# A hybrid encoder block on one core: expert rows gathered as U and V together, in segments of 1, 2, 3 and 2 tiles

## The chip, the cores and the metric

The kernel is one program on one core of a Trainium2 chip, with 128 partitions. Its time is the device time of one execution in microseconds. All data are float32. The engines are called PE (TensorE), DVE (VectorE), ACT (ScalarE), POOL (GpSimd) and SP (SyncE); each takes its own instructions in the order in which they are written, and they wait for each other through semaphores.

## What is computed

One layer on 1024 tokens of 1024 features: a gated linear attention and a sliding-window attention side by side, merged and projected, then a layer that retrieves experts by product keys, a gated embedding add and a last norm. Cut to what matters here:

```python
h = rmsnorm(x, norm_mix)
proj = h @ w_in                       # q, k, v, r, gate of one mixer, q, k, v of the other
x = x + (g_gla * y_gla + g_swa * y_swa) @ w_out
h = rmsnorm(x, norm_ffn)
# 8 heads: top 16 of 128 scores on two sides, top 16 of their 256 sums -> 16 experts e, gates g
u = take(u_tab, e)                    # 16384 x 1024 table
act = gelu(einsum('td,thkd->thk', h, u))
v = take(v_tab, e)                    # 16384 x 1024 table
x = x + einsum('thk,thkd->td', g * act, v)
x = x + sigmoid(rmsnorm(x, norm_ple) @ w_ple_gate) * (p @ w_ple_proj)
return rmsnorm(x, norm_final)
```

Each token takes 8 x 16 = 128 rows of U and 128 rows of V. These rows, 4 KB each, are 1074 MB in all, and each is used once.

## The kernel before

**Tiles, rows and steps.** A tile is 128 tokens, one on each partition; there are eight. For a tile, the k-th expert of a head is one gather of 128 rows (one per partition, 512 KB); a tile has 128 such rows of U and 128 of V. The whole program is laid on one axis of steps n. A step handles two rows, so a head is 8 steps, a tile 64, and all dots are done in steps 0 to 511. Every engine runs a loop over n with its own part of each step.

**A row of experts.** POOL gathers row `at` of U into one of six slots of ubuf and, ten steps later (VLAG), row `at` of V into one of eight slots of vbuf (line 431). DVE multiplies the U row with the tile's normed x in hbuf and sums it into a column of dots (`dot`, line 1133); that frees the slot of U. Once per head, at a step with n % 8 = 0, ACT takes the gelu of all 16 dots (line 877); DVE multiplies them with the gates' softmax (`weights`, line 1141). Ten steps after the dot the V row is added with its weight. Either DVE does it, in acc (line 1159), or PE does: ACT writes the weight on a diagonal (line 885, three buffers) and PE multiplies the diagonal with the V row into ysum in two halves of 512 columns (line 673). ON_PE says which: none in tile 0, the odd rows in tiles 1 to 6, all of tile 7; 512 rows on each. `second_residual` adds acc and ysum to x1 in tX (lines 1170 and 1175), at step 64i+9 for tile i-1.

**The indices** of a head come two heads ahead: `topk` is eleven pieces of DVE work at lines 1068 to 1096, spread over the steps, and ACT's exponential for the gates is at line 873.

**The front.** All before the experts is done for a segment at a time, in stages such as "gv0" (a quarter of v) or "ex1" (the exponentials of a batch of windows). SEGS = (1, 2, 2, 2, 1) tiles. 46 of the 51 weight pieces belong to it, each a slab of 1 MB that SP loads into a ring of three (line 370), PE multiplies with the segment's activations (`by_feature`, line 488, weights stationary; `by_token`, line 497, activations stationary) and ACT evicts from one of two banks (line 700 and others). Each segment loads its slabs anew. `plan()` gives each stage a step: the front of a segment is spread evenly over the steps up to 18 before its first dot, with some stages at least a step behind others (BEHIND). The last stages, wq0 to wq8, project the queries and find the 16 largest scores (`largest`, lines 975 to 981).

**The tail** of a segment (T0, T1, pg0 to pg3, pp, T2; the five other slabs) is the gated embedding add and the last norm. Tails of segments 0, 1 and 2 are hosted in the middle of the front of segments 2, 3 and 4 (HOSTED); those of the last two segments follow their last row, a stage a step.

**Order within step n.** PE: rows of V of step n-10, then the stages of step n. ACT: a gelu of a head if due, the gates' exponential if due, the stages of step n, then diagonals for the next step. DVE: dot, a piece of topk, dot, a piece of topk, the sums of step n-10, the vector parts of the stages of step n-1, weights if due, the norm of the next tile's hbuf (two buffers, line 1120). SP: x1 for hbuf 16 steps ahead of the tile, x1 for tX, then what stages need, then slabs up to step n+2.

## Time and profile before

| what | value |
|---|---|
| median of 3 runs | 3861.61 us (3858.42 to 3883.16) |
| the profiled execution | 3826.47 us |
| its span, first to last instruction | 3824.7 us |
| mean granted TensorE clock | 0.896 of full speed |
| busy: PE, DVE, POOL, ACT | 2919.9, 2603.0, 2337.5, 893.9 us |
| DMA | 1373.44 MB, mean 359 GB/s |

"Busy" counts an engine's instructions, not its waits. A row of a group gives the line, the engine, the operation, what it writes and reads, the count, the busy time and the mean of one, and then the idle time of the engine just before these instructions with what ended it ("issue" is a wait for nothing that the profile shows). The profile counts a float32 matmul twice, so two ysum matmuls of a row stand as four. The DMA share is the mean busy share of the core's sixteen DMA engines; it can go a little over 1, since packets overlap.

### The profile page before, as it was taken

The page shows a single profiled execution, that of the slowest core. Times are in us where ns is not written, and L with a number is a line of the kernel's source. Part 1 is how long each engine was busy: PE and PEld are TensorE (multiplying, and loading weights), DVE is VectorE, ACT ScalarE, POOL GpSimd, SP SyncE. Part 2 cuts the span into 40 slices and gives each one's busy share as a digit, 9 for nine tenths or more (in the row PEclk, how much of TensorE's full clock was granted, in tenths as well). Part 3 has the DMA queues.
Part 4 walks back from the last instruction along what each step waited for, and adds up shares of the span by engine and source line. Part 5 has one row for each costly group of instructions (what it writes and reads, how often), then busy time and mean ns, then how long its engine had stood idle before and what let it go on. Part 6 is the DMA issues. An engine that isn't in the chain of part 4 may idle for free.

```text
span 3824.7 us, 34537 instructions
## 1 busy us (share of the span) xinstructions
PE 2919.9 (76%) x11088; PEld 1913.1 (50%) x11088; DVE 2603.0 (68%) x5403; ACT 893.9 (23%) x1935; POOL 2337.5 (61%) x2052
## 2 busy tenths in 40 slices
...
GB/s 220 221 203 263 388 356 379 313 403 388 382 412 364 381 371 382 318 382 385 385 375 394 389 387 376 342 369 406 395 408 377 412 412 411 399 367 277 397 373 203
DMA packets 342549, 1373.44 MB, mean 359 GB/s; under 512 B 38737, under 2 KB 40657, under 8 KB 309730
## 3 DMA queue, kind: packets, MB, share of 16 engines
q0 software_dynamic: 294912, 1073.87, 72.9%
q1 hardware_dynamic: 47458, 297.36, 19.8%
...
## 4 chain that ended last, share of the span: by engine, by line
PE 16%; POOL 15%; issue 9%; DMA 7%; DVE 3%; another core or an unknown queue 2%; ACT 2%; ACTq 0%; DVEq 0%; POOLq 0%
POOL ubuf L431 8%; POOL vbuf L431 7%; PE ysum L673 7%; DMA vbuf<-in_v,idx 5%; PE bank L488 4%; PE bank L497 3%; DMA ubuf<-in_u,idx 1%; DVE ubuf L1133 1%; PE bank L660 1%; ACT diag L885 1%; DVE acc L1159 0%; PE bank L553 0%; DVE tX L1055 0%; PE wide L505 0%
## 5 line engine op out<-in xcount | busy, mean ns | idle before, releaser
L431 POOL DMA_INDIRECT ubuf<-in_u,idx x1024 | 1175.4, 1148 | 1054.0 <-DVE ubuf L1133 535.2
L673 PE MATMUL ysum<-vbuf,diag 128*128 128x512 f32 x2048 | 1157.2, 708 | 685.3 <-DMA vbuf<-in_v,idx 322.4
L1133 DVE SCALAR_TENSOR_TENSOR ubuf<-ubuf,hbuf 128x1024 f32<-128x1024 f32 x1024 | 1246.8, 1222 | 416.4 <-DMA ubuf<-in_u,idx 339.9
L431 POOL DMA_INDIRECT vbuf<-in_v,idx x1024 | 1161.9, 1135 | 381.7 <-issue 294.0
L673 PEld LDWEIGHTS ysum<-vbuf,diag 128*128 128x128 f32 x2048 | 416.2, 219 | 1309.3 <-issue 923.9
L1159 DVE SCALAR_TENSOR_TENSOR acc<-vbuf,dots,acc 128x1024 f32<-128x1024 f32 x505 | 645.5, 1278 | 62.0 <-DMA vbuf<-in_v,idx 38.5
L488 PE MATMUL bank<-hT,slab 128*128 128x256 f32 (+1 forms) x3680 | 674.5, 343 | 12.1 <-DMA slab<-in_slabs 4.9
L488 PEld LDWEIGHTS bank<-hT,slab 128*128 128x128 f32 x3680 | 601.0, 195 | 118.0 <-issue 55.2
L497 PE MATMUL bank<-slab,hT 128*128 128x256 f32 x1408 | 316.2, 384 | 1.1 <-ACT rE L700 0.8
L497 PEld LDWEIGHTS bank<-slab,hT 128*128 128x128 f32 x1408 | 271.4, 193 | 57.7 <-issue 21.6
L885 ACT ACTIVATE diag<-ident,dots 128x128 f32<-128x128 f32 x512 | 189.6, 394 | 370.3 <-PE ysum L673 148.7
L700 ACT ACTIVATE rA<-bank 128x512 f32<-128x512 f32 (+1 forms) x60 | 30.7, 511 | 475.7 <-PE bank L488 245.3
L700 ACT ACTIVATE rD<-bank 128x512 f32<-128x512 f32 (+1 forms) x60 | 30.7, 512 | 439.8 <-PE bank L488 346.0
L488 PE MATMUL bank<-rC,slab 128*128 128x256 f32 (+1 forms) x640 | 119.6, 347 | 0.0
L497 PE MATMUL bank<-slab,rE 128*128 128x256 f32 x512 | 118.4, 391 | 0.7 <-ACT rE L725 0.7
L488 PEld LDWEIGHTS bank<-rC,slab 128*128 128x128 f32 x640 | 106.6, 198 | 21.0 <-issue 10.8
L497 PE MATMUL bank<-slab,rD 128*128 128x256 f32 x512 | 113.0, 379 | 3.6 <-DVEq L1058 3.6
L488 PE MATMUL bank<-rB,slab 128*128 128x256 f32 (+1 forms) x640 | 113.7, 337 | 0.0
L497 PEld LDWEIGHTS bank<-slab,rE 128*128 128x128 f32 x512 | 101.1, 198 | 23.6 <-issue 8.8
L488 PEld LDWEIGHTS bank<-rB,slab 128*128 128x128 f32 x640 | 102.4, 191 | 15.6 <-issue 6.1
L497 PEld LDWEIGHTS bank<-slab,rD 128*128 128x128 f32 x512 | 97.3, 190 | 22.8 <-issue 5.5
L700 ACT ACTIVATE rB<-bank 128x512 f32<-128x512 f32 (+2 forms) x92 | 49.6, 539 | 209.5 <-PE bank L497 96.6
...
## 6 DMA issues: line engine op xcount, KB each, us to landing
slab<-in_slabs SPq DMA_DIRECT2D x255, 1024.0 KB
ubuf<-in_u,idx POOLq DMA_INDIRECT x1024
vbuf<-in_v,idx POOLq DMA_INDIRECT x1024
rX<-in_x SPq DMA_DIRECT2D x6, 1024.0 KB, 8.6
hbuf<-x_d SPq DMA_DIRECT2D x8, 512.0 KB
tX<-x_d SPq DMA_DIRECT2D x8, 512.0 KB, 10.4
out<-tX SPq DMA_DIRECT2D x8, 512.0 KB
x_d<-rX SPq DMA_DIRECT2D x3, 1024.0 KB, 4.5
```

Source lines behind the costliest of these rows:

```text
L431: nc.gpsimd.indirect_dma_start(out=dst, out_offset=None, in_=rows, in_offset=bass.IndirectOffsetOnAxis(ap=idx[:, b, k:k + 1], axis=0)).the ...
L488: m = mm(b[:, g * tt * P:(g + 1) * tt * P], w[:, k, g * P:g * P + P], src[:, k, 0:tt * P], start=(k == 0), stop=(k == KT - 1))
L497: m = mm(b[:, t * PW:t * PW + PW], src[:, k, t * P:t * P + P], w[:, k, :], start=(k == 0), stop=(k == KT - 1))
L660: m = mm(b, tpT[:, k, t * P:t * P + P], w[:, k, q * 512:q * 512 + 512], start=(k == 0), stop=(k == 1))
L673: ins = mm(ysum[:, c, :], diag[:, m % DS, :], vbuf[:, at % VS, c * 512:c * 512 + 512], start=(m == first), stop=(m == last))
L700: fn(dst, src, kw.pop("func", ACT.Copy), **kw).then_inc(emptied, 1)
L885: fn(diag[:, m % DS, :], ident[:], ACT.Copy, scale=dots[:, g % 3, k:k + 1]).then_inc(diag_done, 1)
L1133: v.scalar_tensor_tensor(out=row, in0=row, scalar=1.0, in1=hbuf[:, i % 2, :], op0=ALU.mult, op1=ALU.mult, accum_out=dots[:, g % 3, k:k + 1 ...
L1159: ins = v.scalar_tensor_tensor(out=acc[:], in0=vbuf[:, at % VS, :], scalar=weight, in1=acc[:], op0=ALU.mult, op1=ALU.add)
```

## The change

The tables U and V stand side by side in memory, so that an expert is one row of 8 KB, and one gather brings both halves into one of eight slots of uv (64 KB per partition, where ubuf and vbuf had 56). The row is dotted, weighed and added from the same slot: dot in step n, gelu and weight of each step's two rows in step n+1, the sum on DVE in step n+1, the diagonal and the sum on PE in step n+2. The 512 gelus (two columns) and weights (two columns) replace 64 of each; the division by the softmax's sum is done two heads ahead (`shares`). The first six rows of each tile are on DVE, then the odd ones of tiles 1 to 7 on PE (427), the others on DVE (597).

The segments are 1, 2, 3 and 2 tiles, each with its own interleaving of stages. A three-tile matmul by feature is 384 columns wide, with a bank for each half. The tails work on groups of tiles (0, 1), (2, 3, 4), (5, 6), (7): the first two are laced into the wq stages of segments 2 and 3, the others follow their last row. Buffers of the front are shared anew, so that x is loaded only after wq8 of the segment before. h is stored to memory and read back for hbuf (now one buffer, HB = 1); acc starts from x1, and x2 is stored and read back for the tail. PE adds the rows that are due ahead of a stage without a slab, or between the halves of one with a slab.

```diff
-SEGS = (1, 2, 2, 2, 1)
+SEGS = (1, 2, 3, 2)
...
-US, VS, DS = 6, 8, 3
+DS = 3
...
+NS = 8
+HB = 1
...
-ON_PE = [(), ODD, ODD, ODD, ODD, ODD, ODD, tuple(range(TOPK))]
+ON_PE = [(), ODD, ODD, ODD, ODD, ODD, ODD, ODD]
+SPARE = 6
...
+GROUPS = ((0, 1), (2, 3, 4), (5, 6), (7,))
+HOST = {0: 2, 1: 3}
...
+    if s in GUEST:
+        names += ["T0", "wq2", "T1", "wq3", "pg0", "wq4", "pg1", "wq5", "pg2", "wq6", "pg3", "wq7", "pp", "wq8", "T2"]
...
+                if at == 1 and n == f"wq{NH}" and s + 1 < NSEG:
+                    sp.wait_ge(bank_full, USES_END[s, n])
                     sp.dma_start(xs[:, 0:SEGS[s + 1], :], x_rows(s + 1)).then_inc(x_in, 16)
...
+                    sp.wait_ge(h_out, 16 * (seg_of(i) + 1))
+                    if i >= HB:
+                        sp.wait_ge(dot_done, (i - HB + 1) * NH * TOPK)
+                    sp.dma_start(hbuf[:, i % HB, :], h_d[i]).then_inc(h_in[i % HB], 16)
+                i, at = divmod(n - 3, PER_TILE)
+                if at == 0 and 1 <= i <= NTILE:
+                    sp.wait_ge(x2_done, i)
+                    sp.dma_start(x2_d[i - 1], acc[:, (i - 1) % 2, :]).then_inc(x2_out[(i - 1) % 2], 16)
...
+            for at in range(ROWS):
+                g, k = divmod(at, TOPK)
+                if k == 0:
+                    pool.wait_ge(idx_ready, g + 1)
+                if at >= NS:
+                    if IS_PE[at - NS]:
+                        pool.wait_ge(v_used_pe, PE_UPTO[at - NS + 1])
+                    else:
+                        pool.wait_ge(v_used_dve, DVE_UPTO[at - NS + 1])
                 nc.gpsimd.indirect_dma_start(
...
+                    out=uv[:, at % NS, :], out_offset=None, in_=a["uv"],
+                    in_offset=bass.IndirectOffsetOnAxis(ap=idx[:, g % 4, k:k + 1], axis=0)
+                    ).then_inc(uv_in[at % NS], 16)
...
             def by_feature(src, tt):
                 w = next_piece()
...
+                for gs in feature_banks(tt):
+                    b = bank_for()
+                    for g in gs:
+                        if g:
+                            add_rows()
...
+                rows_due += [at for at in (2 * (n - 2), 2 * (n - 2) + 1) if 0 <= at < ROWS and IS_PE[at]]
                 for s, name in AT_STEP.get(n, []):
                     stage(s, name)
...
+                add_rows()
...
+            def gelu(n):
+                g, at = divmod(n, STEPS)
+                part = dots[:, g % 3, 2 * at:2 * at + 2]
+                act.wait_ge(dot_done, 2 * n + 2)
+                fn(part, part, ACT.Gelu_apprx_tanh).then_inc(gelu_done, 1)
...
             for n in range(FIRST, LAST + 1):
+                for at in (2 * (n - 2), 2 * (n - 2) + 1):
+                    if 0 <= at < ROWS and IS_PE[at]:
+                        diagonal(at)
+                if 0 <= n - 1 < END:
+                    gelu(n - 1)
...
-                for s, name in AT_STEP.get(n, []):
+                for s, name in AT_STEP.get(n - 1, []):
                     stage(s, name)
...
+                    if at == 0 and 0 <= n - 1 < END:
+                        weights(n - 1)
                     topk_at(n, at)
```

The order of DVE before, in steps 136 and 137 (tile 2), where a head ends: L1133 is a dot, L1159 a sum of a V row ten steps older, L1141 the weights of the whole head.

```order
L1133 SCALAR_TENSOR_TENSOR ubuf,dots<-ubuf,hbuf 128x1024
L1068 TENSOR_TENSOR hot<-vals 128x256
L1133 SCALAR_TENSOR_TENSOR ubuf,dots<-ubuf,hbuf 128x1024
L1074 MAX tv<-hot 128x8
L1159 SCALAR_TENSOR_TENSOR acc<-vbuf,dots,acc 128x1024
L1133 SCALAR_TENSOR_TENSOR ubuf,dots<-ubuf,hbuf 128x1024
L1076 MAX_INDEX pos<-tv,hot 128x8
L1133 SCALAR_TENSOR_TENSOR ubuf,dots<-ubuf,hbuf 128x1024
L1078 MATCH_REPLACE hot<-tv,hot 128x256
L1159 SCALAR_TENSOR_TENSOR acc<-vbuf,dots,acc 128x1024
L1138 RECIPROCAL ginv<-gsum 128x1
L1141 SCALAR_TENSOR_TENSOR dots<-dots,ginv,gexp 128x16
```

The order of DVE after, in steps 137 and 138 (tile 2): L1212 is a dot, L1231 the weights of two rows, L1244 the sum of one of these two rows.

```order
L1212 SCALAR_TENSOR_TENSOR uv,dots<-uv,hbuf 128x1024
L1231 TENSOR_TENSOR dots<-dots,gexp 128x2
L1162 MAX_INDEX pos<-tv,hot 128x8
L1212 SCALAR_TENSOR_TENSOR uv,dots<-uv,hbuf 128x1024
L1164 MATCH_REPLACE hot<-tv,hot 128x256
L1244 SCALAR_TENSOR_TENSOR acc<-uv,dots,acc 128x1024
L1212 SCALAR_TENSOR_TENSOR uv,dots<-uv,hbuf 128x1024
L1231 TENSOR_TENSOR dots<-dots,gexp 128x2
```

The weights now stand between the two dots of every step, and the sum behind them uses the row that the step before dotted.

The order of PE before, in the stages swo of segment 2 (two tiles): L488 is one slab, L673 the ysum matmuls, two for each row.

```order
L673 MATMUL ysum<-vbuf,diag 128x512 x2
L488 MATMUL bank<-rB,slab 128x256 x16
L673 MATMUL ysum<-vbuf,diag 128x512 x4
L488 MATMUL bank<-rB,slab 128x256 x16
L673 MATMUL ysum<-vbuf,diag 128x512 x4
```

The order of PE after, in the stages swo and wo0 of segment 2 (three tiles): L537 is half a slab by feature, L549 matmuls by token.

```order
L537 MATMUL bank<-bufQ,slab 128x384 x8
L728 MATMUL ysum<-uv,diag 128x512 x2
L537 MATMUL bank<-bufQ,slab 128x384 x8
L728 MATMUL ysum<-uv,diag 128x512 x2
L537 MATMUL bank<-bufQ,slab 128x384 x8
L728 MATMUL ysum<-uv,diag 128x512 x2
L537 MATMUL bank<-bufQ,slab 128x384 x8
L728 MATMUL ysum<-uv,diag 128x512 x2
L549 MATMUL bank<-slab,bufC 128x256 x24
```

A row stands between two half slabs, and eight matmuls of 384 columns took the place of eight of 256.

The order of ACT before, beside the stages T2 (hosted), bgg0 and ex0 of segment 2: L885 is a diagonal, L877 the gelu of a head, L873 the gates' exponential, L732 a sigmoid, L738 an exponential.

```order
L877 ACT_TABLE_LOAD
L877 ACTIVATE dots<-dots 128x16
L712 ACT_TABLE_LOAD
L712 ACTIVATE stat_t<-stat_t,eps 128x1
L885 ACTIVATE diag<-ident,dots 128x128 x3
L732 ACT_TABLE_LOAD
L732 ACTIVATE rE<-bank,b_bg 128x256 x2
L885 ACTIVATE diag<-ident,dots 128x128
L873 ACT_TABLE_LOAD
L873 ACTIVATE gexp,gsum<-tv,negmax 128x16
L885 ACTIVATE diag<-ident,dots 128x128
L738 ACTIVATE probs,sm<-rX,sm 128x192 x8
```

The order of ACT after, in a sigmoid and an exponential stage of segment 2: L965 is a diagonal, L957 the gelu of a step, L951 the gates' exponential, L798 a sigmoid, L804 an exponential.

```order
L957 ACTIVATE dots<-dots 128x2
L798 ACT_TABLE_LOAD
L798 ACTIVATE bufE<-bank,b_bg 128x384 x2
L965 ACTIVATE diag<-ident,dots 128x128
L957 ACT_TABLE_LOAD
L957 ACTIVATE dots<-dots 128x2
L965 ACTIVATE diag<-ident,dots 128x128
L957 ACTIVATE dots<-dots 128x2
L951 ACT_TABLE_LOAD
L951 ACTIVATE gexp,gsum<-tv,negmax 128x16
L804 ACTIVATE bufX,sm<-bufX,sm 128x192 x8
L806 ACTIVATE sm<-sm 128x8
```

A gelu stands in every step, ahead of the step's stage, and each stage with a table of its own is followed by a load of the gelu's table.

## Rows read from the trace of the kernel before

**Rows 1.** The page: busy time of the engines; DMA queues with packets, MB, share of sixteen engines.
```profile
PE 2919.9 (76%) x11088; PEld 1913.1 (50%) x11088; DVE 2603.0 (68%) x5403; ACT 893.9 (23%) x1935; POOL 2337.5 (61%) x2052
...
q0 software_dynamic: 294912, 1073.87, 72.9%
q1 hardware_dynamic: 47458, 297.36, 19.8%
```

**Rows 2.** Busy time by stretch: start:end, length, each engine's busy us, PEclk, DMA share, GB/s.
```profile
0.00:282.00 282.00, 240.32 (x1562) 207.85 (x1563) 70.03 (x240) 89.43 (x192) 5.96 (x10) 0.96 0.62 217
282.00:858.00 576.00, 445.36 (x1995) 362.33 (x1994) 471.46 (x977) 136.33 (x271) 315.33 (x281) 0.88 0.90 348
858.00:1729.00 871.00, 691.03 (x2400) 444.81 (x2401) 639.84 (x1339) 206.02 (x450) 586.80 (x509) 0.91 0.97 376
1729.00:3006.00 1277.00, 964.84 (x3406) 602.23 (x3405) 946.13 (x1887) 302.01 (x668) 891.81 (x770) 0.90 0.98 384
3006.00:3401.00 395.00, 258.54 (x972) 146.99 (x970) 302.99 (x626) 66.45 (x151) 288.75 (x251) 0.82 1.02 403
3401.00:3500.00 99.00, 81.31 (x235) 46.37 (x236) 39.56 (x76) 26.26 (x52) 47.98 (x46) 0.88 0.74 262
3500.00:3773.00 273.00, 202.98 (x414) 80.31 (x413) 126.44 (x254) 53.63 (x125) 200.42 (x189) 0.92 0.99 380
3773.00:3824.70 51.70, 35.48 (x111) 22.24 (x109) 6.52 (x8) 13.75 (x27) 0.45 (x1) 0.83 0.24 84
```

**Rows 3.** DVE in order of time: the residual mark of tiles 0, 2 and 5.
```profile
858.23 1.22 DVE L1170 TENSOR_TENSOR tX<-tX,acc 128x1024 f32<-128x1024 f32 x1
...
1729.19 1.22 DVE L1170 TENSOR_TENSOR tX<-tX,acc 128x1024 f32<-128x1024 f32 x1
...
3005.74 1.22 DVE L1170 TENSOR_TENSOR tX<-tX,acc 128x1024 f32<-128x1024 f32 x1
```

**Rows 4.** The DMA in 40 slices of 5 us, from 3200 to 3400 us.
```profile
GB/s 411 410 410 407 411 410 417 407 422 402 415 408 410 423 404 411 409 406 397 401 419 414 408 408 410 411 399 356 306 371 416 412 373 364 355 306 398 373 413 324
```

**Rows 5.** Busy time in three windows, columns as in rows 2.
```profile
1410.00:1482.00 72.00, 64.33 (x241) 45.09 (x242) 50.61 (x84) 13.90 (x30) 47.58 (x40) 1.00 0.94 362
3600.00:3700.00 100.00, 73.49 (x144) 28.78 (x144) 49.56 (x97) 20.01 (x46) 75.25 (x71) 0.91 0.99 371
3000.00:3200.00 200.00, 135.86 (x565) 83.47 (x563) 142.89 (x254) 38.13 (x83) 144.58 (x128) 0.87 1.02 411
```

**Rows 6.** POOL's groups from 3600 to 3700 us: count, busy, mean ns, idle before.
```profile
L431 POOL DMA_INDIRECT ubuf<-in_u,idx x36 | 39.9, 1108 | 11.0 <-issue 11.0
L431 POOL DMA_INDIRECT vbuf<-in_v,idx x35 | 36.1, 1031 | 14.0 <-issue 8.5 <-remote 4.5 <-PE ysum L673 0.9
```

**Rows 7.** PE in order of time, from 1422 us.
```profile
1422.03 3.70 PE L673 MATMUL ysum<-vbuf,diag 128*128 128x512 f32 x8 [0.97 <-ACT diag L885]
1425.57 7.07 PE L488 MATMUL bank<-rB,slab 128*128 128x256 f32 x32
```

**Rows 8.** The page: DMA issues, count, KB, median us to landing.
```profile
rX<-in_x SPq DMA_DIRECT2D x6, 1024.0 KB, 8.6
...
tX<-x_d SPq DMA_DIRECT2D x8, 512.0 KB, 10.4
...
x_d<-rX SPq DMA_DIRECT2D x3, 1024.0 KB, 4.5
```

**Rows 9.** Groups of instructions: count, busy us, mean ns, idle before and releasers.
```profile
L673 PE MATMUL ysum<-vbuf,diag 128*128 128x512 f32 x2048 | 1157.2, 708 | 685.3 <-DMA vbuf<-in_v,idx 322.4 <-ACT diag L885 254.1 <-issue 104.1
L1159 DVE SCALAR_TENSOR_TENSOR acc<-vbuf,dots,acc 128x1024 f32<-128x1024 f32 x505 | 645.5, 1278 | 62.0 <-DMA vbuf<-in_v,idx 38.5 <-issue 15.5
...
L877 ACT ACT_TABLE_LOAD x62 | 79.5, 1283 | 1.1
L1141 DVE SCALAR_TENSOR_TENSOR dots<-dots,ginv,gexp 128x16 f32<-128x16 f32 x64 | 15.0, 235 | 64.9 <-ACT dots L877 49.2 <-issue 10.1
L877 ACT ACTIVATE dots<-dots 128x16 f32<-128x16 f32 x64 | 13.8, 215 | 52.8 <-DVE ubuf L1133 52.2
```

666 lines of the change are left out of this document (337 added, 329 removed).

## Prediction

> **What bounds the kernel now.** I read the page first: its table of engines and its table of DMA queues [rows 1]. No engine is busy for more than 76% of the 3824.7 us. The two DMA queues together are at 92.7% of sixteen engines. The second view is the busy time by stretch [rows 2]. Its borders are the marks of the second residual [rows 3]: this instruction stands at step 64i+9 for tile i-1, so 858 us is step 73, 1729 us step 201, 3006 us step 393. Look at the last column but one: the DMA share is 0.90 up to step 73, then 0.97, 0.98 and 1.02. In its last column the stretches differ: 376, 384, 403 and 380 GB/s with the same full share. So a full share is not yet a fixed rate. The line of rates in fine slices [rows 4] shows a flat top of about 410 GB/s that most slices reach, and dips to 306. I take 412 as the ceiling.
>
> Who makes the dips? At the end, where nothing but gathers runs, 3600:3700 has 371 GB/s [rows 5]. The POOL groups of the same window [rows 6] give 71 gathers, 76.0 us busy, 25.0 us idle, of which only 5.4 us waited for anyone; the rest is the 0.3 us between two issues. One gather thus costs POOL 1.41 us for 0.524 MB, which is 371 GB/s: here POOL sets the pace. The opposite case is 1410:1482, where PE is busy 64.3 of 72 us and the rate falls to 362 GB/s [rows 5]. The order of time there [rows 7] shows why: 7.07 us for one slab of a two-tile segment, then the two ysum rows that waited behind it (3.70 us, and 0.97 us for a diagonal that could not be made earlier). So three things share the bound: bytes at 412 GB/s, POOL's issues where no slab runs, PE where slabs are dense.
>
> **The change, part by part.** The sum goes over the stretches, against the profiled execution of 3826.5 us (span 3824.7); the median of the runs shown, 3861.6, is 1.0092 times that.
>
> Bytes. A gathered pair stays at 1.049 MB (1073.87 MB over 1024, rows 1), 2.10 MB a step. Four segments load 204 slabs in place of 255: 51 x 1.049 = 53.5 MB less. Writing h, writing x2 and reading x2 back are 3 x 4.2 MB, g_ffn three more times 1.6 MB, g_fin once less 0.5 MB. Net about 40 MB less, 97 us at 412 GB/s, if bytes were everything.
>
> POOL. 1024 issues in place of 2048. What an issue of rows of 8 KB costs stands in no row. It lies between one of now (1.1 + 0.3 us) and two of now in one (2.2 + 0.3 us); even the second allows 1.049 MB / 2.5 us = 420 GB/s. I take the first, since both have 128 indices; POOL no longer sets a pace by either end.
>
> Packets of 8 KB. The hardware queue mostly has these, the software queue has 4 KB. By their shares [rows 1] they moved 393 and 385 GB/s per full share; I count nothing for it. The Trainium skill ("DMA: Bandwidth & Descriptors", section "Why small descriptors are slow (HBM only)") gives each packet a fixed overhead of about 3 cycles beside one per 32 bytes; by that, 4 KB to 8 KB is an estimated 1%, and no run here shows it alone. With it the sum below would be some 25 us lower.
>
> Up to step 73 (before: 0 to 282 and 576 us). The front of segment 0 is the same work; one more store and load of h before the first dot, which the 8.6 us of a loaded transfer and less than 5 us of an unloaded one bound [rows 8]: 3 us taken, 285. Then tile 0 with the two-tile front of segment 1, one stage a step. DVE was busy 471 of 576 us, PE 445 [rows 2]. The sums of rows used to start ten steps late and now start one step late: 20 x 1.28 us [rows 9] = 26 us of DVE come in, nothing leaves. Taken: 576 + 26 = 602.
>
> Steps 73 to 201 (before 871 us). Here the front is now three tiles wide, and it still has to fit into 135 steps (54 to 189). A slab takes 7.07 x 1.5 = 10.6 us. There are 46 of them, 488 us. PE's work without ysum and slabs: (2919.9 - 1157.2) / 8 = 220 us a tile, less 51 x 3.54 = 180, leaves 40; three tiles give 119 us. The tail of tiles 0 and 1 is 39 us. Ysum rows: 117 of them, 1.85 us at full clock [rows 7], 2.26 on average (1157.2 / 512, rows 9), 217 to 264 us. Together 863 to 910 us for 135 steps, 6.4 to 6.7 us a step; the DMA needs 328 MB / 412 = 796 us for 128 steps, 6.2 a step. PE becomes the longest. It never filled more than 89% of a window that it bounds [rows 5], so 128 x 6.6 / 0.9 = 939 us, 68 more than before. Bounds: 840 (PE at 97%) and 1010 (PE at 85% with 2.26 us a row and the low clock of rows 2). What takes the edge off is the new rule that rows are added between the halves of a slab.
>
> Steps 201 to 393 (before 1277 us). Segment 3 has two tiles and spreads over 190 steps, a stage every 2.7 steps: PE needs 7.07 + 2.6 x 1.85 = 12 us where the DMA needs (2.7 x 2.10 + 1.05) / 412 = 16.3. Bytes: 403 + 50 + 12 = 465 MB, 1129 us at the ceiling; at 97% of it 1164, and 20 for the fourteen steps in which the tail of three tiles is laced with wq (PE 143 us there, DMA 105, half of it covered by the ring). 1184, 93 less. The longest time for the same bytes is the old 384 GB/s: 1211.
>
> Steps 393 to 512 (before 3006 to 3773, 767 us). 119 steps, 261 MB, 633 us at 412; 20 us for the tail of tiles 5 and 6 at one stage a step, which cost a dip to 262 GB/s in 3401:3500 before, when every row of the last tile was on PE. 653, so 114 less. It holds three gains: POOL's pace is gone, the ten steps of V that ran on alone after the last U are gone, tile 6 has no front.
>
> The ring and the order of waits. Before, U's slot was free after its dot, and V came ten steps later. Now a slot waits for dot, gelu, weights and sum. Gelu (0.22 us, 64 times) becomes 512, and the weights 512 small ones of DVE, 0.13 to 0.24 us each (rows 9 has 0.235 for the old one): 67 to 120 us; 85 more sums on DVE, 109 us. DVE comes to about 2.8 of 3.75 ms, 74%, so it hides this except up to step 73, where 64 small ones are 10 us, inside my 26 us within a factor of two. If the cover is gone, all 109 + 80 us show. Queued behind a weight that waits for ACT are the second dot and the sums, and behind those POOL's next gathers: at most six of eight slots can be in flight, 6.3 MB or 15 us at 412, and about two steps' worth in the steady state. A wait of up to some 7 us is free.
>
> Waits added. One hbuf means that at seven tile borders the load of h can start only after the last dot; a 512 KB load under traffic took 10.4 us [rows 8], and about 7 are covered: 7 x 3.5 = 25 us (bounds 0 and 73). The load of x for segments 2 and 3 now starts a step before it is wanted: 8.6 us and more against 5: 10 us. At the end x2 goes out and comes back (between 4 and 9 us), while the eight V rows that PE still had after the last gather (3773 to 3786) are gone: I count 52 us as before.
>
> Sum: 285 + 602 + 939 + 1184 + 653 + 25 + 10 + 52 = 3750, with the 2 us outside the span 3752, times 1.0092 = **3787 us**, 1.9% less than 3861.6.
>
> **The rivals.**
> Fast: PE keeps up beside three tiles (840), the other stretches run at 98 to 99% of the ceiling (1150, 640), the borders are covered. 285 + 602 + 840 + 1150 + 640 + 10 + 52 + 2 = 3581, 3614 us. For it: rates of 411 over 200 us [rows 5]. Against: PE at 89% cost rate already with two tiles.
>
> No faster gathers: the dips are the DMA's own and not POOL's; then 1211 and 704 (371 GB/s) replace 1184 and 653: 3752 + 78 = 3830, 3865 us, no change. For it: the DMA share was 0.99 in 3600:3700. Against: POOL's idle time there has next to no wait in it.
>
> Slow: ACT's line. Its diagonals, the gelu of each step and the stage's evictions now stand in one queue, and the gelu has its own table. The listing of ACT's instructions has 217 table loads before and 299 now; 82 more at 1.283 us [rows 9] are 105 us. Each of some 190 stages beside gathers also puts at least one eviction (0.6 us) between two gelus, 113 us. From the point where a stage's wait with load and gelu exceeds the 7 us of cover, this stands on the path: 3752 + 218 = 3970, 4006 us, 3.7% slower. For it: DVE waited 49 us for 64 gelus (row of L1141 in [rows 9]), and there are eight times as many now. Against: ACT is busy 23%. The Trainium skill ("ScalarE: Activation LUTs", section "What ACT_TABLE_LOAD costs") adds a drain of about 1.38 us to each load of 1.283: by that this rival would be 113 us worse still. The rows show the 1.283 alone.
>
> **How the numbers follow.** The forecast has 0.42 (its own range 3720 to 3850), the fast case 0.15, no faster gathers 0.17, ACT's line 0.26. Within 1% (about what a measurement of this kernel tells from no change) are the third case and a small part of the first: 0.19. Faster 0.53, slower 0.28. The range reaches far into both outer cases: 3640 to 3970.
>
> **What would show it.** DMA rates near 410 after the last front and POOL waiting for slots instead of issuing; PE over 85% busy between steps 73 and 201 and that stretch longer than 871 us; about 1335 MB in all; seven waits of DVE for hbuf of some 10 us. I am wrong if DVE waits for gelus for more than 150 us in total, if the stretch with the three-tile front is not the slowest per step after tile 0, or if the last stretch stays at 370 GB/s.

## The result and the profile after

| | before | after |
|---|---|---|
| median | 3860.02 us (4 runs, 3849.2 to 3883.16) | 3742.5 us (4 runs, 3738.84 to 3743.41) |
| profiled execution, span | 3826.47, 3824.7 us | 3743.41, 3741.6 us |
| ratio of the medians | | 0.9686, 95% interval 0.9641 to 0.9731 |

The changed kernel is 3.1% faster, 117.5 us. The two profiled executions differ by only 83 us: that of before happened to be 0.9% quicker than its own median, that of after was not.

The page of the changed kernel, engines, packets and DMA queues (before: [rows 1]):

```profile
PE 2810.7 (75%) x9740; PEld 1750.8 (47%) x9740; DVE 2710.1 (72%) x5959; ACT 1067.0 (29%) x2340; POOL 1358.0 (36%) x1028
...
DMA packets 190973, 1333.37 MB, mean 356 GB/s; under 512 B 21697, under 2 KB 23361, under 8 KB 33618
...
q0 software_dynamic: 147456, 1073.81, 70.9%
q1 hardware_dynamic: 43346, 257.51, 17.6%
```

POOL is at 36% in place of 61%, 40 MB are gone, and the software queue moves the same bytes in half as many packets. No engine has moved to the top: PE and DVE are both near three quarters, and the two queues fell from 92.7% to 88.5%.

Busy time by stretch (start:end, length, busy us of PE, PEld, DVE, ACT, POOL, PEclk, DMA share, GB/s). The borders are the dots of steps 0, 73, 201 and 393:

```profile
0.00:332.70 332.70, 273.93 (x1674) 233.42 (x1675) 68.16 (x242) 90.04 (x194) 7.86 (x12) 0.92 0.59 212
332.70:908.40 575.70, 456.65 (x1988) 364.98 (x1987) 487.60 (x1053) 185.97 (x373) 201.16 (x141) 0.88 0.89 350
908.40:1853.50 945.10, 799.83 (x2591) 463.50 (x2590) 698.39 (x1648) 311.94 (x691) 312.87 (x258) 0.92 0.88 350
1853.50:3052.80 1199.30, 885.93 (x2785) 536.62 (x2783) 936.55 (x2023) 331.45 (x737) 497.12 (x384) 0.86 0.95 388
3052.80:3741.60 688.80, 394.40 (x708) 152.30 (x708) 519.36 (x997) 147.57 (x345) 339.00 (x234) 0.75 0.93 384
```

| stretch | before | predicted | after |
|---|---|---|---|
| to the first dot | 281.9 | 285 | 332.7 |
| steps 0 to 73 | 570.3 | 602 | 575.7 |
| steps 73 to 201 | 872.1 | 939 | 945.1 |
| steps 201 to 393 | 1276.8 | 1184 | 1199.3 |
| step 393 to the end | 823.6 | 653 + 52 | 688.8 |
| hbuf borders, loads of x, in the stretches | - | 35 | - |

(The first column is taken between the same dots of the kernel before, so that like stands against like.) The pattern is the predicted one: a loss of 73 us where the front is three tiles wide, gains of 77 and 135 us behind it. What was not foreseen stands in the first line: 51 us lost before the first dot.

What DVE and POOL wait for, from the groups of the page of the changed kernel:

```profile
L492 POOL DMA_INDIRECT uv<-in_uv,idx x1024 | 1357.8, 1326 | 2322.9 <-DVE acc L1244 1245.2
L1212 DVE SCALAR_TENSOR_TENSOR uv<-uv,hbuf 128x1024 f32<-128x1024 f32 x1024 | 1250.4, 1221 | 488.4 <-DMA uv<-in_uv,idx 397.5
...
L1231 DVE TENSOR_TENSOR dots<-dots,gexp 128x2 f32<-128x2 f32 x512 | 80.6, 158 | 132.7 <-ACT dots L957 132.4
L957 ACT ACT_TABLE_LOAD x134 | 171.9, 1283 | 2.3
```

POOL now waits for slots: DVE's sum lets most of them go, and POOL stood idle 1245 us until one of those. DVE waits for rows that have not landed 397.5 us, and for gelus 132.4 us. The flat stretch after the last front, in 40 slices of 5 us from 3060 to 3260 (before: [rows 4]), and the busy time of a window in it and of one at TensorE's limit:

```profile
GB/s 431 429 421 426 431 426 424 434 424 426 428 429 424 429 426 426 424 431 428 424 426 428 428 426 429 423 428 429 424 419 431 418 423 426 429 426 426 428 423 428
```

```profile
3060.00:3310.00 250.00, 146.13 (x203) 45.66 (x203) 214.26 (x431) 51.20 (x129) 151.26 (x101) 0.77 1.01 425
...
1500.00:1550.00 50.00, 50.00 (x208) 39.22 (x207) 23.80 (x44) 9.52 (x24) 13.00 (x11) 1.00 0.76 280
```

There is no dip any more where only gathers run, and the flat top is 425 GB/s, not 412. In 1500:1550 TensorE is busy all 50 us, and the rate falls to 280.

Where the head went. DVE in order of time, and the issues on SP's queue in order of time (start, duration, line):

```profile
332.74 1.23 DVE L1212 SCALAR_TENSOR_TENSOR uv<-uv,hbuf 128x1024 f32<-128x1024 f32 x1 [23.66 <-DMA hbuf<-h_d]
```

```profile
257.97 0.38 SPq L431 DMA_DIRECT2D bufC<-in_x  x1
258.39 68.56 SPq L412 DMA_DIRECT2D slab<-in_slabs  x8
326.99 0.43 SPq L469 DMA_DIRECT2D hbuf<-h_d  x1
```

The first dot waits 23.66 us for its h. The load of h is issued at 326.99 us, since on SP it now stands behind eight slabs, issued over 68.56 us as the ring of slabs lets them go. The kernel before loaded x1 into hbuf 16 steps ahead of the tile, at 214.43 us, and normed it there; the prediction counted only the flight of the new load, not what it is queued behind.

The other 27 us arose earlier. ScalarE's line before and after: the last eviction of segment 0's queries and, after, the first instruction of segment 1, which waits for x. Then both kernels from 100 to 150 us, columns as above:

```profile
242.07 0.38 ACT L700 ACTIVATE rB<-bank 128x256 f32<-128x256 f32 x1 [0.86 <-PE bank L637]
```

```profile
258.03 0.38 ACT L761 ACTIVATE bufE<-bank 128x256 f32<-128x256 f32 x1 [0.86 <-PE bank L697]
268.09 1.06 ACT L768 ACTIVATE bufX<-bufC 128x1024 f32<-128x1024 f32 x1 [9.67 <-DMA bufC<-in_x]
```

```profile
100.00:150.00 50.00, 45.84 (x334) 37.78 (x334) 14.28 (x33) 24.79 (x63) 0.00 (x0) 1.00 0.49 174
100.00:150.00 50.00, 38.58 (x222) 27.77 (x222) 10.88 (x23) 20.55 (x56) 0.00 (x0) 0.83 0.30 105
```

Segment 0's own front ends 16 us later (11 to 12 in the profiles of runs 1, 3, 4, 6 and 8, which have the same front). Part of it is lost here, where TensorE waits twice for VectorE's part of the windowed attention (4.2 and 4.5 us) and the mean granted clock is 0.83 in place of 1.00. Then x of segment 1 is loaded only at 257.97 us, after the last query stage, where it was loaded at 200.77 us before: 10 more. 16 + 10 + 24 is about the 51 us.

### The profile page after: what moved, and what is told of

Read it like the earlier page. It is cut to its first block, busy times and chain, and to the rows that moved or that the text cites. A ratio compares the mean times of both kernels' runs of the same rounds, so it can differ in the third digit from the quotient of the medians.

```text
span 3741.6 us, 32041 instructions
## 1 busy us (share of the span) xinstructions
PE 2810.7 (75%) x9740; PEld 1750.8 (47%) x9740; DVE 2710.1 (72%) x5959; ACT 1067.0 (29%) x2340; POOL 1358.0 (36%) x1028
## 2 busy tenths in 40 slices
DMA packets 190973, 1333.37 MB, mean 356 GB/s; under 512 B 21697, under 2 KB 23361, under 8 KB 33618
## 4 chain that ended last, share of the span: by engine, by line
PE 35%; DMA 29%; DVE 17%; issue 11%; ACT 3%; POOL 3%; SPq 0%; DVEq 0%; POOLq 0%; ACTq 0%
DMA uv<-in_uv,idx 26%; PE bank L537 13%; PE bank L549 12%; DVE acc L1244 6%; PE ysum L728 6%; POOL uv L492 3%; DVE uv L1212 3%; PE bank L608 2%; DMA hbuf<-h_d 2%; DVE lidx L1066 1%; DVE vals L1063 1%; DVE bufX L1031 1%; DMA slab<-in_slabs 1%; ACT bufX L761 1%; PE bank L715 1%
## 5 line engine op out<-in xcount | busy, mean ns | idle before, releaser
L492 POOL DMA_INDIRECT uv<-in_uv,idx x1024 | 1357.8, 1326 | 2322.9 <-DVE acc L1244 1245.2
L1212 DVE SCALAR_TENSOR_TENSOR uv<-uv,hbuf 128x1024 f32<-128x1024 f32 x1024 | 1250.4, 1221 | 488.4 <-DMA uv<-in_uv,idx 397.5
L728 PE MATMUL ysum<-uv,diag 128*128 128x512 f32 x1708 | 1022.8, 733 | 572.1 <-ACT diag L965 567.1
L728 PEld LDWEIGHTS ysum<-uv,diag 128*128 128x128 f32 x1708 | 353.2, 221 | 1119.4 <-ACT diag L965 744.9
L1244 DVE SCALAR_TENSOR_TENSOR acc<-uv,dots,acc 128x1024 f32<-128x1024 f32 x597 | 763.2, 1278 | 10.5 <-DVE acc L1244 1.0
L537 PE MATMUL bank<-bufA,slab 128*128 128x256 f32 (+2 forms) x1920 | 437.6, 385 | 2.0 <-ACT bufB L761 1.7
L965 ACT ACTIVATE diag<-ident,dots 128x128 f32<-128x128 f32 x427 | 170.6, 400 | 849.5 <-DVE dots L1231 845.3
L537 PEld LDWEIGHTS bank<-bufA,slab 128*128 128x128 f32 x1920 | 333.8, 194 | 121.7 <-issue 37.8
L957 ACT ACTIVATE dots<-dots 128x2 f32<-128x2 f32 x512 | 103.6, 202 | 766.9 <-DVE uv L1212 760.8
L549 PE MATMUL bank<-slab,bufA 128*128 128x256 f32 x1408 | 319.9, 386 | 0.7 <-ACT bufE L761 0.4
L549 PEld LDWEIGHTS bank<-slab,bufA 128*128 128x128 f32 x1408 | 273.5, 195 | 62.2 <-issue 25.6
L537 PE MATMUL bank<-bufC,slab 128*128 128x256 f32 (+2 forms) x1024 | 240.6, 393 | 18.8 <-ACT bufE L761 7.1
L537 PEld LDWEIGHTS bank<-bufC,slab 128*128 128x128 f32 x1024 | 181.9, 199 | 77.4 <-issue 31.9
L1231 DVE TENSOR_TENSOR dots<-dots,gexp 128x2 f32<-128x2 f32 x512 | 80.6, 158 | 132.7 <-ACT dots L957 132.4
L537 PE MATMUL bank<-bufQ,slab 128*128 128x256 f32 (+2 forms) x512 | 117.2, 387 | 11.8 <-DMA slab<-in_slabs 11.1
L549 PE MATMUL bank<-slab,bufC 128*128 128x256 f32 x512 | 116.9, 388 | 8.0 <-DVEq L1143 8.0
L537 PE MATMUL bank<-bufB,slab 128*128 128x256 f32 (+2 forms) x512 | 118.0, 388 | 3.5 <-ACT bufE L798 3.5
L549 PE MATMUL bank<-slab,bufQ 128*128 128x256 f32 x512 | 117.0, 387 | 1.9 <-ACT bufE L761 1.2
L549 PEld LDWEIGHTS bank<-slab,bufC 128*128 128x128 f32 x512 | 99.8, 196 | 29.9 <-DVEq L1143 9.5
```

The lines of the kernel that those rows point to most:

```text
L492: nc.gpsimd.indirect_dma_start(out=uv[:, at % NS, :], out_offset=None, in_=a["uv"], in_offset=bass.IndirectOffsetOnAxis(ap=idx[:, g % 4, k ...
L537: m = mm(o, w[:, k, g * P:g * P + P], src(k), start=(k == 0), stop=(k == KT - 1))
L549: m = mm(b[:, c0:c0 + PW], src[:, k, t * P:t * P + P], w[:, k, :], start=(k == 0), stop=(k == KT - 1))
L728: ins = mm(ysum[:, c, :], diag[:, m % DS, :], uv[:, at % NS, D + c * 512:D + c * 512 + 512], start=(m == first), stop=(m == last))
L957: fn(part, part, ACT.Gelu_apprx_tanh).then_inc(gelu_done, 1)
L965: fn(diag[:, m % DS, :], ident[:], ACT.Copy, scale=dots[:, g % 3, k:k + 1]).then_inc(diag_done, 1)
```

## The experiments

Durations of the tiles, from one tile's first dot to the next one's (us, from DVE in order of time), of the kernels that the text below speaks of, with the number of the run. A tile's time starts where its first dot does, after any wait for it, and the tail is what follows the last dot:

```
                 first dot  tile 0     1     2     3     4     5     6     7   tail
before             281.9   516.5  416.4 450.2 427.4 443.3 406.1 404.8 396.7  81.4
after              332.7   517.4  405.8 537.7 378.4 369.5 465.9 325.6 357.1  51.5
1 split            332.0   515.3  424.5 544.2 391.6 400.8 482.9 373.3 387.3  49.3
2 segs             328.0   512.7  390.1 464.6 401.2 467.2 391.5 437.4 336.5  51.7
3 head             304.1   541.1  403.6 539.0 374.2 369.3 467.8 326.7 355.3  49.4
4 spread           327.4   517.6  408.0 480.0 403.7 373.5 397.3 372.1 355.8  49.8
5 halfpe           327.9   520.3  388.2 481.7 376.3 374.4 445.3 325.4 355.9  49.5
6 nogelu           327.9   515.8  407.9 540.0 372.6 370.7 469.0 326.2 354.4  49.3
7 border           327.5   510.9  409.6 529.1 372.1 367.7 456.1 320.5 357.0  49.4
8 ns7              328.3   525.0  432.1 554.7 400.1 411.4 488.4 368.8 388.6  48.7
9 segs10           329.3   511.5  382.8 450.8 392.2 454.9 379.2 429.3 331.2  49.5
10 headspread      304.2   539.7  407.0 482.0 400.6 373.0 396.3 377.2 356.3  49.5
11 balance         304.3   540.7  406.3 476.2 400.8 373.5 399.6 374.7 356.4  49.6
12 segs10spread    327.1   511.9  382.9 402.6 400.9 421.5 393.7 438.4 330.5  51.4
```

Each run's ratio is to runs of the kernel before made beside it; the medians of these were 3850.07 us (runs 1 to 4), 3855.16 (5 to 8), 3826.03 (9 to 11) and 3850.21 (12). "Less" and "more" are against the 3742.5 us of the changed kernel where nothing else is named. Since the kernel before moves by up to 29 us from batch to batch, a difference of some 20 us or less between batches is no result by itself.

**1. The one gather taken apart again** (ring, segments and order as in the changed kernel):

```diff
-                nc.gpsimd.indirect_dma_start(
-                    out=uv[:, at % NS, :], out_offset=None, in_=a["uv"],
...
+                for half, table in enumerate((a["u"], a["v"])):
+                    nc.gpsimd.indirect_dma_start(
+                        out=uv[:, at % NS, half * D:half * D + D], out_offset=None, in_=table,
```

> The changed kernel, but with two gathers of 4 KB rows (from separate tables) for each expert, 2048 issues, everything else as it is. If the pace of POOL's issues (1.41 us for 0.524 MB) and the 4 KB packets made the rate, tile 6 (326 us now, at 412 GB/s) goes back to 2 x 128 x 1.41 = 361 us, the flat top of the rates falls from 427 to about 412, POOL is over 90% occupied there, and the whole is 3743 + 90 to 140 = 3830 to 3880 us. Rival: only the number of bytes and the plan matter; then it stays within 20 us of 3743.

Measured: 3901.5 us, ratio to before 1.0132 (1.0103 to 1.0161). It is 159 us more than the changed kernel, above the upper end of what was expected, and 1.3% more than before. POOL's groups from 3150 to 3350 us, and the window:

```profile
L493 POOL DMA_INDIRECT uv<-in_v,idx x69 | 81.3, 1179 | 21.0 <-issue 21.0
L493 POOL DMA_INDIRECT uv<-in_u,idx x68 | 78.0, 1148 | 20.7 <-issue 20.7
```

```profile
3150.00:3350.00 200.00, 111.70 (x136) 34.12 (x136) 146.10 (x291) 35.40 (x88) 158.53 (x137) 0.65 0.97 357
```

159.3 busy and 41.7 idle, all of it "issue", make up the 200 us: POOL waits for nobody and delivers a gather each 1.46 us, 357 GB/s against 425. That is the pace the prediction read from [rows 6], confirmed. So the joined row is what carries the change: all the rest of it together, without the joined row, is 1.3% slower than before. Run 2 shows the new segments alone on the side of the gains.

**2. Segments as before, the joined row kept.**

```diff
-SEGS = (1, 2, 3, 2)
+SEGS = (1, 2, 2, 2, 1)
-GROUPS = ((0, 1), (2, 3, 4), (5, 6), (7,))
-HOST = {0: 2, 1: 3}
+GROUPS = ((0, 1), (2, 3), (4, 5), (6,), (7,))
+HOST = {0: 2, 1: 3, 2: 4}
```

> The changed kernel with the segments of before (1, 2, 2, 2, 1 tiles; tails of tiles 0-1, 2-3, 4-5 hosted, 6 and 7 at the end): 255 slabs, 53.5 MB more, no three-tile front. If PE is what held the tiles beside the three-tile front and the laced tail, tile 2 falls from 538 to about 440 us, the other tiles pay 53.5 MB / 425 = 126 us of DMA and the total is 3743 + 20 +- 40 us. Rival: bytes bound everywhere, PE never did; then 3743 + 110 to 130.

Measured: 3783.05 us, ratio 0.9824 (0.9796 to 0.9853), 40 us more than the changed kernel, for 54.7 MB more (1388.05 against 1333.37), which at 425 GB/s would be 129 us. By the ratios, too, the two kernels are apart. The saving of bytes is real, and two thirds of it are given back. The places to look are tile 2, beside the end of the three-tile front (537.7 against 464.6 us), and tile 5, beside the three-tile tail (465.9 against 391.5).

**3. The load of the first h ten steps earlier.**

```diff
...
+                if n == -10:
+                    sp.wait_ge(h_out, 16)
+                    sp.dma_start(hbuf[:, 0, :], h_d[0]).then_inc(h_in[0], 16)
...
```

> The changed kernel with the first load of hbuf put on SP's queue at step -10 instead of step 0, where it stood behind slabs that waited for PE until 327 us. If this wait is the 51 us by which the first dot is late, the first dot comes at 270 to 285 us and the whole at 3743 - 30 to 50. Rival: PE's stages of segment 1 set the time of the first steps anyway, and by step 64 no more than 10 us are left of it.

Measured: 3736.24 us, ratio 0.9703 (0.9675 to 0.9731). The first dot comes at 304.1 in place of 332.7, and tile 0 takes 541.1 in place of 517.4 us: 24 of 29 us are given back. The other 5 are no gain of the load either: in runs 2, 4 to 9 and 12, with h as late as in the changed kernel, the first dot comes at 327 to 329 us. By step 6 nothing is left: that dot starts at 369.0 us here and at 368.5 in run 4, where h is late. The start of the dots was late, but segment 1's front, which runs beside tile 0, did not start any earlier, and the first steps wait for that: DVE's longest wait there is 29.4 us, for ScalarE's gelu line, which also carries the stages. This is the rival's case. What still makes this first dot 22 us later than before are segment 0's front, 11 us, and the load of x for segment 1, 10.

**4. The last query slabs and the hosted tails apart.** In segment 2 they come every second step, in segment 3 every fourth, in place of every step.

```diff
-            step = begin + i * (due - begin) // last if i <= last else due + i - last
+            apart = {2: 2, 3: 4}.get(s, 1)
+            step = begin + i * (due - begin) // last if i <= last else due + (i - last) * apart
```

> The changed kernel with the stages wq2 to wq8 and the hosted tail two steps apart in segment 2 and four steps apart in segment 3, instead of one step. If PE (143 us of work in 14 steps beside a DMA that needs 105) made the 210 to 300 GB/s at 1650 to 1800 and 260 at 2850 to 3000 us, tiles 2 and 5 fall from 538 and 466 to about 470 and 400 us, the next front costs some of it, and the whole is 3743 - 90 to 140. Rival: DVE's search for the largest and ACT's line hold these steps by their length, whatever their spacing; then it gains less than 30 us.

Measured: 3686.86 us, ratio 0.9575 (0.9547 to 0.9602): 56 us less, between the two expectations. Two windows of the changed kernel, and the same clock times of this one:

```profile
2850.00:2900.00 50.00, 49.24 (x219) 39.49 (x220) 36.06 (x130) 15.89 (x32) 8.08 (x8) 0.96 0.68 267
2900.00:2950.00 50.00, 50.00 (x220) 40.42 (x219) 30.13 (x107) 13.07 (x24) 9.83 (x10) 1.00 0.71 260
```

```profile
2850.00:2900.00 50.00, 32.82 (x102) 18.36 (x100) 40.57 (x103) 16.35 (x34) 23.25 (x18) 0.83 0.88 352
2900.00:2950.00 50.00, 30.50 (x103) 21.27 (x104) 41.58 (x100) 10.64 (x21) 19.59 (x15) 0.76 1.01 417
```

The same clock times are not the same steps, so here is the whole of tile 5, first of the changed kernel, then of this one:

```profile
2541.50:3007.40 465.90, 349.10 (x1196) 227.57 (x1196) 346.45 (x837) 123.81 (x250) 167.62 (x128) 0.86 0.90 367
```

```profile
2510.20:2907.50 397.30, 266.47 (x812) 160.02 (x812) 307.59 (x666) 103.27 (x234) 168.72 (x128) 0.83 0.97 396
```

TensorE was full in the dense place at 260 to 267 GB/s. Spread out, 83 us of its work have left tile 5, and the tile runs at 396 GB/s. Tiles 2 and 5 lose 58 and 69 us, and tiles 3 and 6, where the work went, take back 25 and 47. TensorE is not the only thing that changed: the seven waits for h at the borders fall from 52.0 to 24.9 us, the one before tile 3 from 10.8 to none. The run does not part the two.

**5. Half of TensorE's slab work gone in three-tile stages.** Four of a slab's eight k blocks are multiplied; the other half of these products is left out. Only one segment has three tiles, the one whose front runs beside tiles 1 and 2; beside tile 5 only the five slabs of the three-tile tail are halved, and the "two three-tile segments" of the text below are these.

```diff
-                        for k in range(KT):
+                        ks = KT // 2 if tt == 3 else KT
+                        for k in range(ks):
```

> Every slab of the two three-tile segments multiplies only the first half of its eight k blocks (the other half of these products is left out); all transfers stay. Theory 'TensorE bounds the steps beside a three-tile front' (stretches of the changed kernel with TensorE busy 49 to 50 us of 50 at 210 to 380 GB/s): tile 2, 537.7 us from its first dot to the next tile's, falls to about 430, tile 5 from 465.9 to about 400, and some of it comes back in tiles 3 and 6; in all 3743 - 110 = about 3635 us (3600 to 3680). Rival 'the DMA engines bound them too': under 40 us less, 3705 to 3745, with the rate unchanged.

Measured: 3642.85 us, ratio 0.9459 (0.94 to 0.9518), 100 us less, with every transfer in place. So TensorE does bound there, as the theory says. Tile 2's time, 1256 to 1794 us, of the changed kernel; then tile 2 of this one, and two windows in it:

```profile
1256.00:1794.00 538.00, 444.91 (x1433) 260.57 (x1432) 385.20 (x1012) 161.09 (x353) 160.32 (x130) 0.92 0.84 332
```

```profile
1236.40:1718.10 481.70, 342.66 (x1033) 191.54 (x1032) 384.28 (x1012) 161.79 (x353) 168.29 (x130) 0.85 0.92 370
...
1600.00:1650.00 50.00, 48.82 (x198) 34.82 (x197) 48.33 (x198) 18.85 (x34) 12.36 (x11) 1.00 0.94 369
1650.00:1700.00 50.00, 33.20 (x105) 18.51 (x105) 47.54 (x183) 14.68 (x28) 13.70 (x11) 0.85 0.78 291
```

TensorE has 102 us less to do in tile 2, and the tile is 56 us shorter: 481.7 us, not 430. Tile 5 fell to 445.3 and not to 400. What holds the rest of tile 2's excess this run does not say. There are two candidates in the rows of its last query stages: TensorE is still busy 48.8 of 50 us in one window, and VectorE, which searches for the largest scores there, 48.3 and 47.5 of 50 us.

**6. Gelu without its table.** A plain copy in its place; the gelu is left out.

```diff
-                fn(part, part, ACT.Gelu_apprx_tanh).then_inc(gelu_done, 1)
+                fn(part, part, ACT.Copy).then_inc(gelu_done, 1)
```

> A plain copy takes the place of the gelu (gelu is left out), so the 134 table loads of 1283 ns go; bytes and instructions stay. Theory 'ScalarE's line is off the path': under 15 us less, 3728 to 3745, though VectorE's waits for the dots' line go. Rival (the slow case of the prediction): the table loads delay evictions that TensorE waits for, 134 x 1.283 = 172 us of them, of which half counts: 80 us less or more, under 3665.

Measured: 3733.69 us, ratio 0.9694 (0.9648 to 0.974), 9 us less, which is no more than batches differ by; from the first dot to the end the two profiled executions took 3408.9 and 3406.0 us. More loads are gone than was expected: 108 are left of 299, since other functions need theirs less often too. So 191 loads or 245 us of ScalarE's time are out, and next to nothing of them was on the path. DVE's wait for this line stays at 104.9 of 132.4 us:

```profile
L1231 DVE TENSOR_TENSOR dots<-dots,gexp 128x2 f32<-128x2 f32 x512 | 80.3, 157 | 105.0 <-ACT dots L957 104.9
```

So most of the wait is not the tables, and the slow rival falls as far as they carried it; its evictions were not taken out by any run.

**7. No h at the borders.** Every tile's dots use the h of tile 0; the other seven are neither loaded nor waited for, so the right h is left out.

```diff
-                if at == 0 and 0 <= i < NTILE:
+                if at == 0 and i == 0:
...
-                if at % (NH * TOPK) == 0:
+                if at == 0:
```

> h is loaded for tile 0 alone and every later tile's dots use tile 0's h (the right h is left out), so the seven waits at the borders between tiles, 52 us in all in the profile of the changed kernel (2 to 12 us each), go, with 14 MB less moved (28 of 2 MB... 7 x 2 MB, about 33 us at 425 GB/s where the rate binds). Theory 'the ring of eight slots covers a border': 10 to 35 us less, all of it the bytes. Rival 'a border stops the line': 52 us of waits and the bytes, 60 to 85 us less.

The bytes in this text are wrong: an h is 512 KB, so seven are 3.7 MB, 9 us at 425 GB/s. Measured: 3703.71 us, ratio 0.9619 (0.9574 to 0.9664), 39 us less. The seven waits were 52.0 us in the profile (75.7 less the first one's 23.7), so some 30 of 52 us stood on the path (from the first dot to the end the profiled executions differ by 36 us). With the bytes put right, the rival's sum would be about 61 and the theory's at most 9; 39 lies between them, nearer to "a border stops the line". The ring covers some 20 of the 52 us.

**8. Seven slots.**

```diff
-NS = 8
+NS = 7
```

> Seven slots in the ring in place of eight. Theory 'the engines' queue holds the gathers, not the ring': eight gathers of 1 MB are 20 us of transfers at 425 GB/s and seven are 17, both longer than a gather's flight; 0 to 15 us more. Rival 'the ring is what feeds the queue': a slot fewer lowers the rate in the quiet stretches from 425 to about 400 GB/s and costs 40 us or more.

Measured: 3949.67 us, ratio 1.0256 (1.0207 to 1.0305), 207 us more. That is the rival's side, "40 us or more", by five times its number, and the rate fell to 375 GB/s and not to 400. The theory, that the engines' queue holds the gathers and the ring has room to spare, falls. Busy time of the gathers' own stretch in tile 7:

```profile
3650.00:3700.00 50.00, 26.14 (x37) 8.32 (x36) 39.45 (x84) 8.77 (x24) 24.87 (x18) 0.78 0.97 376
3700.00:3750.00 50.00, 27.87 (x36) 9.01 (x36) 37.49 (x74) 11.02 (x25) 23.37 (x18) 0.70 0.97 374
```

36 gathers in 100 us are 2.78 us each; seven are 19.4 us. With eight slots 101 gathers took 250 us (window above): 2.475 each, eight are 19.8. So a slot's turn, from gather to gather, takes the same time of 19.4 to 19.8 us in both, and with seven slots that turn sets the pace. With eight, the turn and the transfers meet at 425 GB/s, with nothing between them. The DMA share hardly tells the two apart: it is 0.97 here at 375 GB/s and 1.01 there at 425, and 0.97 in run 1, where POOL set the pace at 357. A share near 1 does not show by itself that the transfers bind. DVE's waits for rows rise from 397.5 to 675.3 us, and every tile is longer, the first by 8 us, the others by 17 to 43.

**9. Ten slots.** With segments of two tiles five buffers of the front are 4 KB per partition smaller, 20 KB in all; two more slots take 16. As run 2, with:

```diff
-NS = 8
+NS = 10
```

> Segments of 1, 2, 2, 2, 1 tiles again (3783.05 us with eight slots) and ten slots in the ring, which the space of the smaller buffers gives. Theory 'the ring limits, one turn of it takes about 19.6 us' (eight slots: 425 GB/s; seven slots: 374 to 376, both 19.6 us a turn): the quiet stretches can't rise far, since the DMA engines' share is 1.01 there, but every stretch below 400 GB/s gains from two more slots: 100 to 180 us less than segs, 3600 to 3680. Rival 'eight slots are enough, and only fewer hurt': within 30 us of segs, 3750 to 3785.

Measured: 3713.03 us, ratio 0.9686 (0.9616 to 0.9755), 70 us less than with eight by the medians, 53 by the ratios, since the kernel before was quicker in this batch. Between the two expectations; the direction is the ring's. The window of run 2 and two of this one where no slab runs:

```profile
3500.00:3650.00 150.00, 85.39 (x122) 27.06 (x121) 128.25 (x258) 30.18 (x77) 91.55 (x60) 0.78 1.01 421
```

```profile
3400.00:3500.00 100.00, 60.93 (x87) 18.94 (x86) 88.13 (x169) 22.18 (x53) 58.42 (x43) 0.74 1.01 421
3500.00:3600.00 100.00, 58.16 (x80) 18.27 (x78) 83.24 (x159) 17.63 (x47) 56.84 (x40) 0.74 1.01 421
```

421 in all three, at a share of 1.01. There the transfers bind, and two more slots give nothing; a turn of ten takes 24 us then (83 gathers in 200 us). The gain comes from stretches with stages beside them: DVE's waits for rows fall from 522.3 to 399.5 us.

**10. The early h and the spread stages together.** The diffs of runs 3 and 4.

> The early load of h (6 us less alone) and the eighth query slabs and hosted tails two and four steps apart (56 us less alone) together. If they touch different tiles they add up: 3686.86 - 6 = about 3681 us, 3670 to 3690. Rival: the first dot's 23 us come back in full now, 3660 to 3670.

Measured: 3688.87 us, ratio 0.9624 (0.9554 to 0.9693). No more than the spread alone. The first dot comes 23 us earlier than in run 4, and tile 0 takes 22 us more (539.7 against 517.6): as in run 3, the early load gives nothing.

**11. Fewer V rows on TensorE in tiles 1, 2 and 5,** on top of run 10:

```diff
-ON_PE = [(), ODD, ODD, ODD, ODD, ODD, ODD, ODD]
+SIX, FOUR = (1, 3, 5, 9, 11, 13), (1, 5, 9, 13)
+ON_PE = [(), SIX, FOUR, ODD, ODD, SIX, ODD, ODD]
```

> headspread, and TensorE's share of the V rows cut from 8 of 16 to 6 in tiles 1 and 5 and to 4 in tile 2; VectorE takes the 64 rows (32 of them in tile 2, 1.28 us each). Theory 'TensorE bounds there': tiles 1, 2 and 5 give 10 to 40 us together, 3640 to 3670. Rival 'VectorE or the ring bounds as well': no less than headspread, since VectorE has 41 us more in tile 2 and a slot is let go later: 3680 to 3710.

Measured: 3684.14 us (3680.03 to 3684.86) against 3688.87 (3683.64 to 3691.92) in the same batch, 4.7 us less, the rival's range; tile 2 is 6 us shorter, tile 5 is 3 longer. TensorE's busy time fell by 44 us in tile 2 (404.8 to 361.1 us) without the time following: once the stages are apart, TensorE's sum over the tile no longer sets its time. Whether its dense places, VectorE with 38 us more work, or the ring does, the run does not say.

**12. Ten slots, two-tile segments, stages apart.** Run 9 with the last query slabs and hosted tails of segments 2 and 3 two steps apart.

```diff
-            step = begin + i * (due - begin) // last if i <= last else due + i - last
+            apart = {2:2,3:2}.get(s, 1)
+            step = begin + i * (due - begin) // last if i <= last else due + (i - last) * apart
```

> segs10 with the last query slabs and the hosted tails of segments 2 and 3 two steps apart. If what helped the three-tile version in its tile 2 (537.7 to 480.0 us) and tile 5 (465.9 to 397.3) helps here, tiles 2 and 4 (450.8 and 454.9 us) come to about 410 each, a third of it goes back to their neighbours, and it takes 3713 - 50 = about 3660 us (3640 to 3690), the fastest of all. Rival: with segments of two tiles the stacked steps are short and ten slots cover them, so within 15 us of segs10, 3700 to 3725.

Measured: 3659.09 us (3656.76 to 3662.6), ratio 0.9498 (0.9472 to 0.9524), the fastest of the kernels that compute everything: 5.0% below before and 83 us below the changed kernel, with the segments of before. The expectation held: tile 2 fell from 450.8 to 402.6 us and tile 4 from 454.9 to 421.5, and tiles 3, 5 and 6 took 9 to 15 us back each. Its tile 2 (1222 to 1625 us) and tile 4:

```profile
1222.00:1625.00 403.00, 321.01 (x1152) 215.40 (x1151) 328.38 (x760) 128.76 (x278) 168.99 (x131) 0.90 1.01 415
2026.00:2448.00 422.00, 344.48 (x1292) 236.67 (x1290) 335.74 (x779) 138.55 (x307) 163.36 (x130) 0.92 0.99 404
```

Tile 2 runs at 415 GB/s and a full share, with TensorE busy 80%. It moves 54.7 MB more than the changed kernel and is faster all the same.

## Why the prediction was right, and where it was not

The forecast was 3787 us and 1.9% less; 3742.5 and 3.1% less were measured, inside the likeliest case's range of 3720 to 3850, near its lower end. The mechanism was right where it mattered most, the pace of POOL's issues and TensorE beside three tiles. That the sum came within 44.5 us is in part luck: its terms were off by up to 48 us in both directions. Point by point:

- **POOL's pace** [rows 6]: right, and the largest part. Run 1 prices it at 159 us for the new arrangement. What an issue of 8 KB rows costs was open between 1.4 and 2.5 us; its mean is 1.326 us busy, with 0.35 us to the next where it waits for nothing (174.4 us in 492 times). The rival "no faster gathers" falls.
- **Steps 73 to 201**: 939 predicted, 945.1 measured, TensorE busy 84.6% of it, just short of the stated "over 85%". Run 5 confirms that TensorE bounds there: the stretch falls to 867.3 us. The even pace that the term assumed is not what happened: in tile 1 there was no loss (405.8 against 416.4 us), and all of it stands in tile 2, where the last query slabs and the hosted tail come one a step. "It never filled more than 89% of a window" held for the window shown and not in general: the kernel before has one of 46.0 in 50 us (2400:2450), and the changed kernel fills 50 of 50 in places. That 945 came so near to 939 is luck.
- **Steps 201 to 393 and the end**: 1184 and 705 predicted, 1199.3 and 688.8 measured. The ceiling of 412 GB/s was too low: 425 where only gathers run. The higher ceiling and the dearer dense stages nearly cancelled. (The Trainium skill, "HBM Reference", "Specifications (TRN2)", gives about 425 GB/s for a core that streams alone; the trace of after agrees, that of before did not show it.) The stacked stages that the prediction priced at 20 us each cost more: putting them apart (run 4) gave 56 us in all, in the stretches before and behind step 201 together.
- **Packets**: nothing counted. The ceiling rose from about 410 [rows 4] to 425. The rule of the Trainium skill ("DMA: Bandwidth & Descriptors", "Why small descriptors are slow (HBM only)") points the same way, with an estimated 1%; 3% was measured between two kernels that differ in more than the packet. Run 1 has 4 KB packets but is paced by POOL, so none of the runs separates the two. The bytes per full share that the prediction compared [rows 1] cannot do it either: with packets of 8 KB in both, that figure of the software queue is 405 GB/s in the changed kernel and 387 in run 8.
- **The head**: 285 predicted, 332.7 measured. Here a step failed, in three places. "The front of segment 0 is the same work" was wrong by 16 us, 11 to 12 in other runs: in the new order TensorE waits more. Of the loads of x that now come late the prediction counted those for segments 2 and 3 and not the one for segment 1, 10 us. And of the load of h it took 3 us for the flight; it is late by its place in SP's queue, and DVE waits 24 us for it. Runs 3 and 10 show that these 24 us cost nothing: with h there, the first steps wait for segment 1's front instead. So about half of the 51 us count.
- **Steps 0 to 73**: 602 predicted, 575.7 measured, 5 more than before. This does not show that the sums which start earlier were free, since the stretch begins behind the 24 us wait for h, while segment 1's front went on; without that wait (run 3) the same stretch takes 599.4 us. Taken together, the head and this stretch were predicted at 887 us and took 908.4, against 852.2 before. At step 12, where the earlier sums are all done, the changed kernel is 23 us behind (419.6 against 396.6 us), no more than the late front. It loses the other 33 between steps 12 and 73, 7 of them at the border to tile 1. What makes the rest no run shows; DVE's waits for ACT's gelus are 25.7 us there, and 4.8 before. The prediction's number for this stretch fits run 3, but not by the sums it named.
- **The borders**: 25 predicted, about 30 of 52 us of waits shown by run 7. The size was right. The sentence ahead of it, "a wait of up to some 7 us is free", was not: run 8 shows a turn of 19.4 to 19.8 us that eight slots only just fill.
- **ACT's line**: run 6 gives 9 us at most for all the table loads that the gelu brings. The trace had 132.4 us of waits, near the stated limit of 150, and 105 of them stayed without the tables. The rival's other half, evictions between two gelus, was left in place by every run.
- **The scale**: the sum of the terms was 3752, the profiled execution took 3743.4. Multiplying by 1.0092 added 35 us; it carried the difference between two executions of the kernel before over to another kernel. It is most of the 44.5 us between forecast and result; the errors of the terms (+48, -26, +6, +15, -16, and -35 for borders and loads that lay inside the stretches) cancel to -8. The first two are not independent: the wait for h moves 24 us from one to the other.

Open: what holds the rest of tile 2's excess when TensorE's slab work is halved, what makes the 26 us between steps 12 and 73, and how much of 412 to 425 is the packet and how much the absence of other transfers.
